# First three projections of layer 0 in contraction halves, modulation sums row by row on VectorE, two PSUM readers moved to ScalarE

## What is computed

```python
for l in range(DEPTH):
    sh1, sc1, gt1, sh2, sc2, gt2 = split(silu(cond) @ w_mod[l] + b_mod[l], 6)   # cond: c_ctx or c
    h = rmsnorm(x, g_mix[l]) * (1 + sc1) + sh1
    aq, ak, av, mq, mk, mv, mo, mi, mf = split(h @ w_in[l])
    att = attention(rmsnorm(aq), rmsnorm(ak), av)           # latent: rotary, plus 128 cached keys
    b = cumsum(log_sigmoid(mf)); u = mi - b                 # both directions
    M = cummax(u) (and the start state)                     # running-max stabiliser
    # decay of key s at query t: exp(u[s] - M[t]), kept for s <= t (or s >= t)
    h_ml = mLSTM(mq, mk, mv, decays, state_C, state_n, state_m)
    x = x + gt1 * (concat(att, sigmoid(mo) * rmsnorm(h_ml)) @ w_out[l])
    h = rmsnorm(x, g_ffn[l]) * (1 + sc2) + sh2
    x = x + gt2 * moe(h)                                    # 16 experts, top 2 in the top group
```

## Time and profile before

| | us |
|---|---|
| median of 3 runs | 792.28 (791.99 to 792.37) |
| the profiled execution's own time | 794.9 |
| its span, first to last instruction | 793.0 |
| PE busy | 759.5 (96%) |
| VectorE busy | 329.3 (42%) |
| ScalarE busy | 158.2 (20%) |
| POOL busy | 56.6 (7%) |
| moved by DMA | 289.41 MB, mean 365 GB/s |

### The profile page before, as it was taken

One profiled execution on the slowest core, in us unless ns is written; L12 is line 12 of the kernel. 1 busy time (PEld: TensorE's weight loads), 2 busy tenths in 40 slices (PEclk: granted clock), 3 DMA queues, 4 the chain that ended last, 5 costly groups with the idle time before them and its releaser, 6 DMA issues.

```text
span 793.0 us, 10913 instructions
## 1 busy us (share of the span) xinstructions
PE 759.5 (96%) x4683; PEld 401.3 (51%) x4683; DVE 329.3 (42%) x534; ACT 158.2 (20%) x355; POOL 56.6 (7%) x69
## 2 busy tenths in 40 slices
PE   3799999999999999999899999999899999999997
PEld 2265556786534433444245646688653444344423
DVE  0279566714323232123228965772431323213223
ACT  2301114602212012020012111361221201102001
POOL 0040052101100000000000004200110000000000
PEclk9999999999999999999999999999999999999999
DMA  8999907999999999999999970579889999999993
GB/s 346 403 378 374 375 7 295 413 362 424 426 420 424 423 421 425 426 419 423 422 407 407 380 301 0 218 289 397 326 328 400 427 426 418 424 426 419 426 421 152
DMA packets 49858, 289.41 MB, mean 365 GB/s; under 512 B 3401, under 2 KB 5761, under 8 KB 23697
## 3 DMA queue, kind: packets, MB, share of 16 engines
q1 hardware_dynamic: 48080, 285.30, 88.6%
q0 software_dynamic: 1488, 3.31, 1.2%
q10 hardware_dynamic: 240, 0.08, 0.0%
HBM read 286.31 MB, written 2.37 MB: 364 GB/s over the span
## 4 chain that ended last, share of the span: by engine, by line
PE 83%; DMA 13%; DVE 2%; SPq 1%; ACT 1%; issue 0%; ACTq 0%; DVEq 0%
PE ps L1100 22%; PE ps L764 16%; PE ps L1130 12%; DMA ring<-in_w_e_up 9%; PE ps L1014 7%; PE ps L1084 4%; DMA ring<-in_w_in 4%; PE ps L778 4%; PE ps L639 3%; PE ps L1145 2%; PE ps L1112 1%; PE ps L1155 1%; PE ps L892 1%; PE ps L917 1%; PE ps L947 1%; DVE xT L1654 1%
## 5 line engine op out<-in xcount | busy, mean ns | idle before, releaser
L1100 PE MATMUL ps<-ring,xe 128*64 128x512 f32 x688 | 151.8, 594 | 4.0 <-DMA ring<-in_w_e_up 4.0
L764 PE MATMUL ps<-ring,hT 128*128 128x512 f32 (+1 forms) x320 | 128.7, 564 | 2.0 <-DMA ring<-in_w_in 2.0
L1100 PEld LDWEIGHTS ps<-ring,xe 128*64 128x64 f32 x688 | 48.5, 137 | 105.3 <-issue 99.8
L764 PEld LDWEIGHTS ps<-ring,hT 128*128 128x128 f32 x320 | 62.1, 196 | 65.2 <-issue 59.5
L1130 PE MATMUL ps<-ring,ex 128*32 128x512 f32 x736 | 92.0, 594 | 0.2 <-issue 0.2
L1995 DVE COPY ye<-ps 64x512 f32<-64x512 f32 (+1 forms) x28 | 19.3, 689 | 164.2 <-PE ps L1130 164.1
L1014 PE MATMUL ps<-hT,ring 128*128 128x256 f32 x256 | 57.1, 381 | 0.0
L1979 DVE RECIPROCAL ex<-ex 128x512 f32<-128x512 f32 x16 | 53.6, 3353 | 0.6
L1130 PEld LDWEIGHTS ps<-ring,ex 128*32 128x32 f32 x736 | 26.0, 110 | 52.1 <-issue 49.4
L1977 DVE TENSOR_SCALAR ex<-ex 128x512 f32<-128x512 f32 x16 | 6.8, 427 | 109.4 <-ACT ex L1528 109.4
L1014 PEld LDWEIGHTS ps<-hT,ring 128*128 128x128 f32 x256 | 48.0, 190 | 7.2 <-issue 0.8
(11 more groups left out here) (272 smaller groups left out, 803.6 us busy)
## 6 DMA issues: line engine op xcount, KB each, us to landing
ring<-in_w_mod SPq DMA_DIRECT2D x24, 2048.0 KB, 19.1
ring<-in_w_e_up SPq DMA_DIRECT2D x23, 2048.0 KB, 20.0
ring<-in_w_e_gate SPq DMA_DIRECT2D x20, 2048.0 KB, 22.3
ring<-in_w_e_down SPq DMA_DIRECT2D x19, 2048.0 KB, 23.2
ring<-in_w_in SPq DMA_DIRECT2D x10, 2048.0 KB, 23.4
beside<-in_w_e_gate SPq DMA_DIRECT2D x8, 2048.0 KB, 25.5
beside<-in_w_e_down SPq DMA_DIRECT2D x7, 2048.0 KB, 19.8
beside<-in_w_e_up SPq DMA_DIRECT2D x5, 2048.0 KB, 18.1
```

Of the source, the lines that this page charges most:

```text
L764: mm = pe.matmul(bank[:, 0:width], hT[:, k, b * P:(b + 1) * P], w[:, k, :], start=(k == 0), stop=(k == KD - 1))
L1100: mm = pe.matmul(bank[PLACES * j:PLACES * j + PLACES, :], xe[:, k, c:c + PLACES], w[:, j, i, :], start=(k == 0), stop=(k == KD - 1))
```

## The change

- Layer 0's first section is cut in two of two slots each, by features: section (0,-1) holds columns 0 to 511 of shift and of scale (chunks 0 to 3 of `hT`), section (0,0) columns 512 to 1023. A slot holds all eight rows k of its 512 columns. `feature_rows` makes 32 matmuls of 128 columns per slot, `feature_columns` the constants of four chunks.
- `mk`, `mq` and `mv` of layer 0 are loaded in two halves of 1 MB, k = 0 to 3 and k = 4 to 7, and projected in the same halves: the three front halves, with `feature_rows(0)` and its columns between them, then the three back halves. Their banks stay open in between; `mv` moves to banks 4 and 5.
- Loads: x goes ahead of all `w_mod`; then section (0,-1), the front halves, section (0,0), the back halves, aq, akv, mod 0, mod 1, mo, mod 2, mod 3. Layer 1 keeps its order.
- DVE's sums go by rows: in layer 0 rows 0 and 1 before the scans, row 2 behind them, rows 3 to 7 behind the copy of the scan columns and ahead of the akv copies. In layer 1 the turns are those of before.
- ACT copies `mq` out of PSUM, and takes each decay block as Relu(max row - column) with a negated column `start` that DVE writes.
- PE: twelve `warm` matmuls at the start; x is turned ahead of the parameter rows; `scatter_pair` of the last pair of layer 0 comes behind the `If` of the spill instead of ahead of it.

```diff
+SECTION_CHUNKS[0, -1], SECTION_CHUNKS[0, 0] = (0, 8), (4, 8)
+HALVED = ("mk", "mq", "mv")
-BETWEEN = {"mk": (0,), "mq": (1, 2), "mv": (3,)}
-SUM_TURNS = (((0, 1, 2), (3,), ()), ((0, 1, 2), (3,), ()))
+BETWEEN = ({"akv": (0, 1), "mo": (2, 3)}, {"mk": (0,), "mq": (1, 2), "mv": (3,)})
+SUM_TURNS = (((0, 1), (2,), (3, 4, 5, 6, 7)), (tuple(range(6)), (6, 7), ()))
...
+                if l == 0 and g == "mv":
+                    put((("mv", b), 0), 4 + b)
...
-            load_section(0, 0, 0)
             sp.dma_start(cst[:, 0:P], t["constants"][:, 0:P]).then_inc(const_in, 16)
             for b, name in enumerate(("x_prompt", "x_sample")):
                 sp.dma_start(xtok[:, b, :], t[name][0]).then_inc(x_in, 16)
-            load_section(0, 0, 1, 2, 3)
...
+            load_features(-1)
+            for g, landed in zip(HALVED, front_in):
+                if weights[g, 0][0] == RING - 1:
+                    taken(sp, ("x", 0), ("x", 1), ("x", 2), ("x", 3))
+                load_rows(g, slice(0, KD // 2), landed)
+            load_features(0)
+            for g in HALVED:
+                load_rows(g, slice(KD // 2, KD), slot_landed[weights[g, 0][0]])
...
+            def feature_rows(s, *which):
+                bank = begin(("modrow", 0, s)) if 0 in which else ps[banks["modrow", 0, s][0]]
+                for v in which:
+                    w = landed(("mod", 0, s, v)).rearrange("p (k n) -> p k n", k=KD)
+                    for k in range(KD):
+                        for g in range(4):
+                            mm = pe.matmul(bank[32 * g:32 * g + 32, v * P:(v + 1) * P], cT[:, NB * k:NB * k + 32],
+                                           w[:, k, g * P:(g + 1) * P], start=(k == 0), stop=(k == KD - 1))
...
                 if l == 0:
+                    for b in range(NB):
+                        norm_parts(l, b)
                     pe.wait_ge(cond_silu, 1)
-                    section_rows(0, 0, 0)
+                    feature_rows(-1, 0)
+                    for b in range(NB):
+                        norm_total(l, b)
+                    feature_rows(-1, 1)
+                    warm((("mk", 0), l), 3)
+                    section_columns(0, -1)
+                    warm((("mk", 0), l), 3)
+                    warm((("mk", 0), l), 3)
...
+                if l == 0:
+                    front, back = range(0, KD // 2), range(KD // 2, KD)
+                    project("mk", fresh=True, ks=front)
+                    project_turned("mq", range(NB), front)
+                    feature_rows(0, 0, 1)
+                    project("mv", (0,), ks=front)
+                    section_columns(0, 0)
+                    project("mv", (1,), ks=front)
+                    project("mk", fresh=True, ks=back)
+                    project_turned("mq", (0,), back)
+                    gates()
+                    project_turned("mq", (1,), back)
+                    gate_rows()
+                    project("mv", ks=back)
...
-                if l + 1 < DEPTH:
-                    scatter_pair(PAIRS - 1, 0, KD)
                 with pe.If(limit[0] > SLOTS):
...
-                if l + 1 == DEPTH:
-                    scatter_pair(PAIRS - 1, 0, KD)
+                scatter_pair(PAIRS - 1, 0, KD)
...
 (ScalarE, behind log1p, and in decay(d))
+                for i in range(2):
+                    key = (("mq", i), l)
+                    bank = full(act, key)
+                    act.activation(mqT[:, :, 2 * i:2 * i + 2, :]..., bank..., ACT.Copy).then_inc(free(key), 1)
...
+                    for i in range(2):
+                        key = (("mrow", d, i), l)
+                        bank = full(act, key)
+                        for j in range(2):
+                            for b in range(NB):
+                                h, c = 2 * i + j, j * TOK + b * P
+                                ins = act.activation(W[:, d, h, b, :], bank[:, c:c + P], ACT.Relu,
+                                                     bias=start[:, b, d * MH + h:d * MH + h + 1])
+                        ins.then_inc(free(key), 1)
...
 (VectorE, behind the scans)
-                    dve.tensor_copy(mqT[:, :, 2 * i:2 * i + 2, :]..., bank...).then_inc(free(key), 1)
                 section_sums(l, 1, SUM_TURNS[l][1])
                 key = ("scanT", l)
                 ...
-                gaps(0)
+                dve.tensor_scalar(start[:, :, :], qc[:, :, 0, :], -1.0, None, ALU.mult).then_inc(start_ready, 1)
                 section_sums(l, 1, SUM_TURNS[l][2])
...
-                gaps(1)
...
 (POOL, ahead of the gate weights' loads)
-            pool.wait_ge(slot_landed[weights["mk", 0][0]], 16)
+            pool.wait_ge(front_in[0], 16)
```

More of the change, by code:

```diff
@@ L248, in put @@
         order.append(slot)
-    for i in range(section_slots(0, 0)):
-        put(("mod", 0, 0, i))
+    for s in (-1, 0):
+        for i in range(section_slots(0, s)):
+            put(("mod", 0, s, i))
+    for g in HALVED:
+        put((g, 0))
     for l in range(DEPTH):
         for g in PROJ:
-            put((g, l))
-            for i in BETWEEN.get(g, ()):
+            if l > 0 or g not in HALVED:
+                put((g, l))
+            for i in BETWEEN[l].get(g, ()):
                 put(("mod", l, 1, i))
@@ L706, in raw_logits @@
                             done((("logits", b), l), mm)
+            pe.wait_ge(ones_set, 3)
+            warm(("x", 0), 12)
             pe.wait_ge(const_in, 16)
[L709 to L713, removed]
             pe.wait_ge(x_in, 16 * NB)
@@ L721, in _ @@
                 done(("x", r), mm)
+            pe.wait_ge(rows_in, 16 * ROW_LOADS * DEPTH)
+            for l in range(DEPTH):
+                bank = begin(("rows", l))
+                done(("rows", l), pe.transpose(bank[:, 0:ROWS_L], rowsin[:, l, :], ident[0:ROWS_L, 0:ROWS_L]))
             def section_sums(l, s):
                 bank = begin(("modrow", l, s))
-                pe.wait_ge(sum_step, SUM_STEPS * (l + 1))
+                for k in range(SUM_ROWS[l], KD):
+                    w = landed(("mod", l, s, k // 2)).rearrange("p (k n) -> p k n", k=2)
+                    for g in range(4):
+                        pe.matmul(bank[32 * g:32 * g + 32, :], cT[:, NB * k:NB * k + 32], w[:, k % 2, g * 512:(g + 1) * 512],
+                                  start=(k == SUM_ROWS[l]), stop=False)
+                pe.wait_ge(sum_step, sum_steps(l + 1))
                 for b in range(NB):
@@ L1391, in _ @@
                 act.activation(rows[:, 2, :, :], rows[:, 2, :, :], ACT.Ln, bias=1.0).then_inc(log1p, 1)
+                for i in range(2):
+                    key = (("mq", i), l)
+                    bank = full(act, key)
+                    act.activation(mqT[:, :, 2 * i:2 * i + 2, :].rearrange("p b h t -> p h b t"),
+                                   bank[:, :].rearrange("p (h b t) -> p h b t", h=2, b=NB), ACT.Copy).then_inc(free(key), 1)
                 act.wait_ge(scan_diff, l + 1)
@@ L1718, in _ @@
                 ins.then_inc(scan_diff, 1)
-                for i in range(2):
-                    key = (("mq", i), l)
-                    bank = full(dve, key)
-                    dve.tensor_copy(mqT[:, :, 2 * i:2 * i + 2, :].rearrange("p b h t -> p h b t"),
-                                    bank[:, :].rearrange("p (h b t) -> p h b t", h=2, b=NB)).then_inc(free(key), 1)
                 section_sums(l, 1, SUM_TURNS[l][1])
```

188 lines of the change are left out of this document (113 added, 75 removed).

## The result

The changed kernel takes 797.28 us (median of 4 runs, 796.82 to 798.81), the kernel before, beside it, 792.33 (791.99 to 792.61): ratio 1.0056, 95% interval 1.0039 to 1.0072. It is slower by 4.95 us by the medians (3.1 to 5.7 by the interval). The forecast of 788.4 was wrong in sign and in range.

What follows compares the result with a forecast made beforehand. Layer 0 was seen as a relay: PE sets when slots come free, then bytes set the end. Front gain 6.6 less tail 3.6 leaves 3.0; DMA makes it 3.8, plus 0.1: 788.4 us, range 783.8 to 791.9 with rivals 1 and 2.

Steps and rivals of the forecast that it cites:

- mk's front: Start of layer 0: mk's front half would start at 23.4 us, 10.7 us earlier than before.
- aq's end: End of the aq projection (a): 6.6 us earlier, from 93.46 to 86.9, with half the clock loss regained.
- the sums' pitch of 2.26 and their end: VectorE behind aq: ten multiply-adds, one every 2.26 us, 22.6 us in all, from a+1.2 to a+23.8.
- the 0.9 us that the DMA side and the `If` were to give together: End of layer 0: DMA stream gains 3.8 us where PE is early by 3.0; moving the `If` gives 0.1.
- Rival 4: mk and mq front halves: clock stays low, 12.9 us more than forecast, 801.3 us; chance 0.05.
- rival 3: Start: loads issued together land together, so the change does not start earlier, 793.4 us; chance 0.06.
- Rival 2: Behind aq: late sum or alternating ACT, DVE and POOL lengthen the tail; 3 us more gives 791.4; chance 0.12.
- 8.0 us of normalising and turning: VectorE behind the sums and root: 8.0 us as in the earlier profile, putting the keys at a+36.2.
- come behind its squares anyway: POOL behind aq: its masks come after its squares anyway, so moving decay blocks to ACT costs nothing there.
- The terms are differences: Whole kernel: 3.9 us taken off the profiled 794.9 gives 791.0, and off the median 792.28 gives 788.4.
- the loss behind aq: From aq's end to the cross scores: five rows on VectorE delay them from a+39.3, giving back 3.6 us.
- the second slot: Start, section (0,-1): PE comes to the second slot at 19.3 us, by x's path; each slot takes 2.1.

Runs made afterwards that it cites:

- experiment 1: The kernel before, unchanged, profiled a second time: 793.43 us, ratio 1.0009; its profiled execution had none of the earlier profile's clock dips.
- experiment 6: The change with ScalarE's layer 0 gate copies ahead of its root: 797.03 us; with POOL's masks and gate additions also behind the keys: 798.18 us.
- experiment 2: The change with rows 3 to 7 of layer 0 summed over 2 of 2048 columns: 3170.71 us, tokens going to other experts; cross scores at a+37.65.
- ScalarE's part alone: The kernel before with only the mq copies and decay blocks moved to ScalarE: 792.99 us, ratio 0.9995.
- experiments 3: The change with row 2 moved into the tail, six rows there in place of five: 802.40 us, ratio 1.0129.
- 9, the change again: The changed kernel as it is, run again beside even turns on the same chip: 797.69 us, ratio 1.0061.
- even turns: The change with section (0,1) loads earlier and layer 0 rows summed as 0 to 2, 3 and 4, 5 to 7: 788.08 us, ratio 0.9950.
- experiment 4: The change with POOL's two decay masks ahead of its squares: 799.03 us, ratio 1.0068.
- experiment 5: The change with POOL's masks and gate additions of layer 0 waiting for the finished keys: 796.18 us, ratio 1.0043.
- experiment 8: The change with section (0,1) loads earlier and rows summed 0 to 3, 4 and 5, 6 and 7: 792.90 us; with masks ahead of squares: 793.33 us.

## Why the prediction was wrong

**Held.** mk's front at 24.04 (23.4 forecast) at full clock; aq's end at 87.59 (86.9); the sums' pitch of 2.26 and their end; the 6.9 us from the keys to the cross scores (6.8); the DMA pause mostly filled and the `over` load at 171.23; the last stage's 4 us of DMA wait; layer 1 of equal length up to its last down matmuls, 358.2 us from mk in experiment 1 and 358.1 in the change; the 0.9 us that the DMA side and the `If` were to give together (the lag of 4.2 at the cross scores is 3.3 at layer 1's start; no run separates the two). Rival 4, a low clock in the front halves, did not come, nor did rival 3. Rival 2, that the tail costs more, is what came; but not by its mechanism, the alternating chain, which experiment 6 shows to be covered.

**Failed.** Three terms, taken against -3.9:

1. *"then 8.0 us of normalising and turning ... Keys at a+36.2."* They came at a+39.7, and the cross scores at a+46.64 instead of a+42.9 (39.3 + 3.6): 3.7 us, of which 3.4 are the 11.4 us that this stretch took. I took the 8.0 us from a stretch that had only the end of POOL's masks and one `og` addition beside it. In the change nearly all that POOL does behind its squares lies beside it, and without POOL it takes 5.9. I had written that the masks "come behind its squares anyway", and put their cost at nothing. This is the largest term, and one to one on the path.
2. *"The terms are differences, so 794.9 becomes 791.0 and the median 788.4."* The difference was taken between a forecast without clock dips and an execution of before that had some. Experiment 1 shows the stretch from the start to the cross scores 2.75 us shorter. Against it, the loss behind aq should have been 42.9 - 37.6 = 5.3, not 3.6, and the gain ahead of it 5.5, not 6.6. By this alone the forecast is -1.1 us, no change that can be measured.
3. The front: aq's end 0.7 later than forecast, and 0.6 of it arises before mk's front half. PE came to the second slot at 19.92 and not at 19.3, behind a first slot that took 3.46 us instead of 2.1, with the granted clock at 0.69 from 14 to 16 us and 0.50 from 16 to 18; the terms that I list there add up to 18.7, so even the 19.3 was no sum of them. From mk's front half to aq's end it took 63.55 us, as forecast, but by two errors that cancel: a wait of 1.28 us for the second slot of section (0,0), at 41.64, was not in my sum, and the clock gave back all of its loss where I had counted half.

Together -3.9 + 3.7 + 2.75 + 0.7 = +3.3, which is the lag at layer 1's start. The profiled executions end 4.3 us apart (spans 790.6 and 794.9), the medians 5.0. The last microsecond arises in the last 18 us, at the last down matmuls and the last scatter of layer 1, here in the change:

```profile
777.53 7.34 PE L1216 MATMUL ps<-ring,ex 128*32 128x512 f32 x64
785.62 2.06 PE L1241 MATMUL ps<-lists,ye 64*128 64x128 f32 x32 [0.75 <-issue]
```

From the one start to the other it takes 8.09 us, and 7.01 in experiment 1, where the scatter follows without a gap. Eight of the ten profiles of the change and its variants (experiment 2 left out) have such a gap, of 0.65 to 1.11 us, with nothing in the profile that PE waits for; the kernel before, in both profiles, and ScalarE's part alone have none. So it looks like a cost of the change, though the two without it (experiments 3 and 9, the change again) show that it does not come each time. Its cause stays open. The forecast had no term for it.

The range failed with the terms. It had nothing for clock dips in the execution that the differences were taken from, though the prediction names the 0.93 of that stage. And it gave the tail 1.5 us to either side, where what POOL costs VectorE could have been seen in the earlier trace rows itself: those 3.27 us hold two products of 640 elements, and an addition as large takes 0.83 there.

## What to carry to other kernels

Price work that is moved onto an engine by where it will stand, not by how idle the engine is: the same rows cost 9 us behind aq in the change (46.64 - 37.65) and nothing in even turns, which differs by two tuples, the order of four loads and the turns of the sums. When such work slides a stretch of VectorE along in time, look which operations of GpSimd will then lie beside it, and where VectorE's operation reads two tensors from SBUF, price each pair as one after the other. And take differences from an execution near the median: check the granted clock in every stretch that a term uses.

## What the runs showed of the hardware

A multiply-add of 128x2048 on VectorE with two tensors from SBUF took 4.45 us instead of 2.34 beside a GpSimd product of 128x1024, and two such products took 8.74 instead of 4.66 (experiment 4): each side lost nearly the other's whole time. A reciprocal with one tensor lost nothing beside the same products, nor did they (3.35 and 4.68 us, experiment 5).

Where TensorE waited about 2 us for the scan columns, ahead of `max_rows`, the granted clock then went to 0.50: it was 0.50 from 92 to 96 us and 0.53 to 98 in the first kernel of experiment 8, and 0.50 from 90 to 96 and 0.80 to 98 in the second. The wait of 1.7 us more thus came with 3.3 us more of matmul time in the first. With the usual wait of 0.41 us in the same place the clock fell in one of twelve profiles, the one that the prediction used (0.70 from 96 to 98 us, 0.50 to 100), and in no other.
